# Sixteen modulation tiles per layer change their DMA queue: from SyncE's to ScalarE's, inside the attention of the two mixing layers

## The reference, cut to what matters

```python
c_act = silu(c)
for l in range(2):
    mod = c_act @ w_ada[l] + b_ada[l]                  # (1, 6*1024)
    sh1, sc1, g1, sh2, sc2, g2 = split(mod, 6)
    h = rms_norm(x, norm1_g[l]) * (1 + sc1) + sh1
    q, k, v, iq, ik, iw, z, xbc, dt_raw, ga, gm = split(h @ w_in[l])
    o_attn = dsa_attention(rope(rms(q)), rope(rms(k)), v, iq, ik, iw, 64) @ w_attn_o[l]
    o_ssm = gated_rms(ssd_scan(...)) @ w_ssm_o[l]
    x = x + g1 * ((sigmoid(ga) * o_attn + sigmoid(gm) * o_ssm) @ w_out[l])
    h = rms_norm(x, norm2_g[l]) * (1 + sc2) + sh2
    ...
    x = x + g2 * (ffn(h) @ w_down[l])
```

## Time and profile before

| | |
|---|---|
| three runs | 1649.43, 1653.10, 1655.61 us; median 1653.1 us |
| profiled execution | 1655.45 us, of it span 1653.8 us |
| TensorE / GpSimd / VectorE / ScalarE busy | 96% / 77% / 56% / 52% |
| attention of layer 0, layer 1 (pair 0 to the last transposes) | about 355 to 432 us, 998 to 1070 us from the start |

### The profile page before, as it was taken

The page is one execution under the profiler, slowest core; times in us unless marked ns, Lnnn a source line. Parts: engine busy times, 40 slices in busy tenths (PEclk is TensorE's granted clock), DMA queues, the critical chain, the costliest instruction groups (busy, mean ns, idle before and its releaser), DMA issues.

```text
span 1653.8 us, 33845 instructions
## 1 busy us (share of the span) xinstructions
PE 1593.0 (96%) x13182; PEld 1541.0 (93%) x13182; DVE 925.4 (56%) x1799; ACT 866.3 (52%) x1432; POOL 1271.9 (77%) x948
## 2 busy tenths in 40 slices
PE   7999999999999999999999899999999999999999
PEld 6999988898999999999998899999999998799999
DVE  7767777567646763467677757754442256632200
ACT  3554555554456663465455564545664455655532
POOL 1878967675779999678986767697998786279996
PEclk7999999999999999999999999999999999999999
DMA  8545744446446657455764545654665664146654
GB/s 306 178 146 204 244 165 160 142 166 242 166 141 235 235 200 255 149 156 174 242 207 144 164 155 192 231 178 148 184 190 174 200 202 142 47 152 192 183 188 128
DMA packets 85518, 302.23 MB, mean 183 GB/s; under 512 B 9840, under 2 KB 12528, under 8 KB 85104
## 3 DMA queue, kind: packets, MB, share of 16 engines
q1 hardware_dynamic: 85360, 300.06, 55.3%
HBM read 298.98 MB, written 1.05 MB: 181 GB/s over the span
## 4 chain that ended last, share of the span: by engine, by line
PE 71%; DVE 11%; ACT 5%; DVEq 4%; issue 3%; POOL 2%; DMA 2%; SPq 1%; ACTq 0%; POOLq 0%
PE gemm_bank L1688 63%; ACT w_hi L443 2%; POOL w_lo L425 2%; PE turn_bank L1871 2%; PE turn_bank L1842 2%; DVEq L1337 2%; DVE ada_acc L848 1%; DVE conv L848 1%; DVE h_lo L1383 1%; DVE idx_score L848 1%; DMA ada_first<-in_w_ada 1%; DVE probs L1045 1%; DVEq L1221 1%; PE outp_bank L2078 1%; PE score_bank L1688 1%
## 5 line engine op out<-in xcount | busy, mean ns | idle before, releaser
L425 POOL TENSOR_TENSOR w_lo<-w_raw,w_hi 128x512 fp32r<-128x512 f32 x944 | 1271.7, 1377 | 370.7 <-ACT w_hi L443 357.8
L443 ACT ACTIVATE w_hi<-w_raw 128x1024 fp32r<-128x1024 f32 x472 | 491.7, 1046 | 590.6 <-PE gemm_bank L1688 517.5
L1688 PE MATMUL gemm_bank<-h_hi,w_hi 128*128 128x256 f32 (+1 forms) x2144 | 608.8, 284 | 7.2 <-DVE conv L848 3.7
L1688 PE MATMUL gemm_bank<-h_hi,w_lo 128*128 128x256 f32 (+1 forms) x2144 | 601.2, 280 | 0.0
L1688 PE MATMUL gemm_bank<-h_lo,w_hi 128*128 128x256 f32 (+1 forms) x2144 | 600.8, 280 | 0.0
L1688 PEld LDWEIGHTS gemm_bank<-h_hi,w_hi 128*128 128x128 f32 (+1 forms) x2144 | 403.9, 188 | 16.2 <-issue 7.4
L1688 PEld LDWEIGHTS gemm_bank<-h_lo,w_hi 128*128 128x128 f32 (+1 forms) x2144 | 404.5, 189 | 0.3
L1688 PEld LDWEIGHTS gemm_bank<-h_hi,w_lo 128*128 128x128 f32 (+1 forms) x2144 | 404.0, 188 | 0.2
L848 DVE SCALAR_TENSOR_TENSOR conv<-gemm_bank,params_sb,conv 128x255 f32<-128x255 f32 (+1 forms) x320 | 139.5, 477 | 161.9 <-ACT conv L774 110.7
L1688 PE MATMUL gemm_bank<-w_hi,h_hi 128*128 128x256 f32 (+1 forms) x672 | 193.5, 288 | 2.7 <-DVE h_lo L848 1.5
L1688 PE MATMUL gemm_bank<-w_lo,h_hi 128*128 128x256 f32 (+1 forms) x672 | 188.0, 280 | 0.0
(11 more groups left out here) (310 smaller groups left out, 2165.2 us busy)
## 6 DMA issues: line engine op xcount, KB each, us to landing
w_raw<-in_stream SPq DMA_DIRECT2D x458, 512.0 KB, 3.8
ada_w<-in_w_ada SPq DMA_DIRECT2D x80, 512.0 KB, 4.6
ada_first<-in_w_ada SPq DMA_DIRECT2D x16, 512.0 KB, 12.1
w_raw<-in_stream SPq DMA_DIRECT2D x8, 256.0 KB, 3.1
alibi_sb<-in_alibi SPq DMA_DIRECT2D x1, 1920.0 KB, 7.8
residual<-in_x_t SPq DMA_DIRECT2D x1, 1024.0 KB, 6.7
ada_acc<-in_rows SPq DMA_DIRECT2D x1, 1024.0 KB, 5.1
out_x<-residual SPq DMA_DIRECT2D x4, 256.0 KB, 4.6
```

The costliest lines, as they stand in the source:

```text
L425: ins = nc.gpsimd.tensor_tensor(w_lo[:, s, e], w_raw[:, s, e], w_hi[:, s, e].bitcast(f32), ALU.subtract)
L443: A(w_hi[:, s, 0:n], w_raw[:, s, 0:n], ACT.Copy).then_inc(hi_ready, 1)
L1688: ins = M(o, a, b, start=first and i == 0, stop=last and i == len(passes) - 1, skip_group_check=True)
```

## The change

The sixteen tiles leave SyncE's list and are loaded by ScalarE, two for each pair. The wait that protects the buffer (`ada_used`) goes with each load and now stands in ScalarE's in-order list. Tile 0 is loaded at the head of pair 0, tile 2p+1 at the head of pair p, and tile 2p+2 behind `turn_evac` of pair p (p up to 6). The other tiles of a layer stay on SyncE. Nothing else is changed: same tiles, same buffers, same order of use.

```diff
@@ ada_slots (SyncE's list) @@
             slots = [((U_Z + i, 0), ada_tile(l, "scan", i)) for i in range(8)]
             slots += [(scan_part(h), ada_tile(l, "scan", 8 + h // 4)) for h in range(2, 32, 4)]
-            slots += [(SO_ORDER[min(h, 13)], ada_tile(l, "attention", h)) for h in range(16)]
@@ ScalarE @@
+            def load_attention_tile(l, h):
+                i = ada_tile(l, "attention", h)
+                act.wait_ge(ada_used, i - 1)
+                nc.scalar.dma_start(ada_w[:, i % 2, :], w_ada[i]).then_inc(ada_full[i % 2], 16)
+
             def attention(l):
                 t0 = T_AT if l < DEPTH else T2_AT
                 for p in range(HEADS // 2):
+                    if l < DEPTH:
+                        if p == 0:
+                            load_attention_tile(l, 0)
+                        load_attention_tile(l, 2 * p + 1)
                     head_exp(l, 2 * p)
                     head_exp(l, 2 * p + 1)
...
                     turn_evac(l, 2 * p, t0)
+                    if l < DEPTH and p < 7:
+                        load_attention_tile(l, 2 * p + 2)
```

## The result

The change makes the kernel slower: 1670.03 us (median of four runs, 1668.93 to 1673.64) against 1651.26 us (median of four, 1648.99 to 1655.61), a ratio of 1.0098, 95% interval 1.0064 to 1.0132. The forecast was 1658.0 in a range of 1646 to 1665, made from the first three runs of before (median 1653.1); the time lies beyond it. Of the cases written down, "Clearly slower" (1665) is the nearest.

What follows compares the result with a forecast made beforehand. The prediction took TensorE, busy for 96% of the span, to bound the kernel. Delays of +2.8 us in layer 0 and +2.1 in layer 1 made +4.9, moving the median from 1653.1 to 1658.0 us, range 1646 to 1665.

Steps and rivals of the forecast that it cites:

- Clearly slower: Rival: ScalarE's tiles share DMA engines with freed chunks and take 5 us or more; +12 us, 1665; chance 0.13.
- D: The start of a pair's head maxima on VectorE; the next pair's scores were taken to follow 1.93 us later.
- SyncE's waits go, and give nothing: Both layers: freed chunks win at most TensorE's 0.64 and 1.66 us, swallowed by its wait for the maxima.
- Pair 0 costs nothing: Pair 0: tile 0 lands at about 355.7, wanted from 357.37; cost zero, with 1.7 us to spare.
- The load leaves at D + 0.4: Later pairs: the even tile's load is issued behind the 0.49 us copy `turn_evac`, at about D + 0.4.
- The tile is there 3.8 us after its issue, and only the even tile of a pair counts: Later pairs: tile there at D + 4.2, wanted at D + 2.57; a 1.6 us stall where VectorE starts in time.
- DMA queues: Rule that a second issuing engine saves only issue time: sum 0; kept as a rival, 1653 us, chance 0.12.
- Pair 3 to D of pair 4: No idle time follows pair 3, so D of pair 4 moves +1.1 us in layer 0, +1.6 in layer 1.
- Pairs 1 and 2 take the stall up: VectorE's idle time before D of pair 3, 2.53 and 1.68 us, absorbs the stall; cost 0.
- Pairs 4 to 6: Pair 4: 0; pair 5: 0 in layer 0, +0.4 in layer 1; pair 6 in layer 0: stall 1.6, accumulations +1.0.
- ScalarE's issues: Two issues ahead of a pair's exponentials, 0.8 to 1.7 us, cost 0; as a rival +10 us, 1663, chance 0.05.
- Clock: Within the 0.13 rival: a longer wait lets TensorE's clock fall for a chunk, 2.7 us.

Runs made afterwards that it cites:

- four_act: The change with four tile buffers instead of two, ScalarE asking for tiles a pair ahead; ratio 0.9965 to the kernel before.
- four_sp: The kernel before, tiles still in SyncE's list, with the same four tile buffers in the attention; ratio 0.9968 to the kernel before.
- held_chunks: The change, with SyncE loading six chunks of each attention only once a pair of tiles has landed; ratio 1.0054 to the kernel before.

## Why the prediction was wrong, step by step

Where the two attentions grew, as a change of the time from one D to the next (from the first D to tile 14 in all; one profiled execution each):

| us | pair 0 | pairs 1, 2 | pair 3 | pairs 4 to 6 | behind D of pair 7 | sum |
|---|---|---|---|---|---|---|
| layer 0, forecast | 0 | 0 | +1.1 | +2.6 | -0.9 | +2.8 |
| layer 0, measured | -2.65 | +1.23 | +4.35 | +4.10 | -0.91 | +6.12 |
| layer 1, forecast | 0 | 0 | +1.6 | +0.5 | 0 | +2.1 |
| layer 1, measured | +2.75 | +0.90 | +2.11 | +5.24 | +2.90 | +13.90 |

- **SyncE's waits go, and give nothing.** Right. The 8.40 and 2.04 us of ScalarE went. TensorE's waits for `probsT` of 0.64 and 1.66 us in pair 3 went too, and nothing came of it, since it then waits for the maxima.
- **Pair 0 costs nothing.** Right: tiles 0 and 1 landed in 3.2 and 4.7 us, no wait but for `y_low`, as before.
- **The load leaves at D + 0.4.** Half a microsecond too late: it left at 389.11, with D at 389.21. The issue went out with the start of the copy ahead of it (389.10), not its end. By itself this made the sum too large.
- **The tile is there 3.8 us after its issue, and only the even tile of a pair counts.** This is the step that failed. The 3.8 came from sixteen loads that SyncE had spaced out. On ScalarE two leave 0.4 us apart, together with the chunks that the list now lets go; tiles 2 to 13 landed in 3.6 us at the median in both layers before, and in 4.7 (layer 0) and 5.0 (layer 1) after, with 9.8 and 7.7 at the worst. With it goes something that I left out: of the two tiles of a pair I worked out only the even one, and put the odd one at nothing without a reason. The odd one lands later still, at 5.3 and 6.1 us at the median, and its waits of 3.55 and 3.10 us (before 399.35, and before tile 13 at 1073.13) are as large as any. Over both attentions VectorE waited 24.0 us for tiles, 16.8 for even and 7.2 for odd ones; in the change's second execution 16.2 and 5.4. The run with half the bytes ties size to cause: with landings near my figure the loss was 6.8 us, not 16 to 19.
- **DMA queues.** The Trainium skill (DMA: Bandwidth & Descriptors, Issuing engines are not separate DMA queues) says that loads issued by different engines interleave on the same sixteen DMA engines. The longer landings agree. The time that it would give, no change, holds for four_act and four_sp, 0.9965 and 0.9968, where the asking is equally early on either queue; where the move also changes when a tile is asked for, it doesn't.
- **Pair 3 to D of pair 4.** The right place, +1.1 and +1.6 us forecast; +4.35 in layer 0 (13.2 against 8.9) and +2.1 in layer 1 (10.5 against 8.4). The even tile did what the sum says: there at D + 4.4 and D + 4.0 (forecast D + 4.2), it cost 2.05 and 1.65 us (forecast 1.6), though only because the earlier issue made up for the longer landing. The gap in layer 0 is the odd tile, 3.55 us, and belongs to this execution: in the change's second one tile 7 landed in 5.6 us, cost 0.48, and the next D came 9.5 us after, not 13.2. The accumulations took 3.4 us there, 1.15 less than before where I took 0.5; in layer 1 4.6, 0.6 more. VectorE's timeline of layer 1, tiles 6 and 7, then 13:

```profile
1043.27 4.62 DVE L858 SCALAR_TENSOR_TENSOR ada_acc<-ada_w,c_act,ada_acc 128x1024 f32<-128x1024 f32 x2 [1.65 <-DMA ada_w<-in_w_ada]
...
1073.13 1.28 DVE L858 SCALAR_TENSOR_TENSOR ada_acc<-ada_w,c_act,ada_acc 128x1024 f32<-128x1024 f32 x1 [3.10 <-DMA ada_w<-in_w_ada]
```

- **Pairs 1 and 2 take the stall up.** Right for pair 2: it grew by 0.1 us in either layer, and 3.33 us of VectorE's idle time were left before D of pair 3 in layer 0. Wrong for pair 1, which let 1.1 and 0.8 us through: its tiles landed in 5.9 and 7.0 us in layer 0 and in 4.8 and 6.0 in layer 1.
- **Pairs 4 to 6**: D of pair 4 to D of pair 7 was forecast to grow by 2.6 us in layer 0, all in pair 6, and 0.5 in layer 1, mostly in pair 5. It grew from 19.7 to 23.8 (+4.1) and from 20.0 to 25.3 (+5.2), in all three pairs, by 1.0 to 2.0 us each (pair 5 +1.7 and +2.0, where I had put 0 and 0.4).
- **Pair 0 in the table** is not the change's: the low clock that follows the wait for `y_low` came in layer 0 before and in layer 1 after. The two cancel in the sum of 20.0.
- **Behind D of pair 7** layer 0 came out as forecast. In layer 1 TensorE waited 2.84 us for `probsT`, whose copy stood behind tile 13 and its 3.10 us, and ran at the lower clock from 1078.63 on.
- **ScalarE's issues.** Right: 0.33 us each at the median. The exponentials started 0.85 us after D in pair 3, no later than their maxima allowed.
- **Clock.** I had it as a rival, with 0.13. In the two profiled executions of before and after 9.2 us of the 20.0 are longer busy time of TensorE. It is a step that my sum set to nothing for the likeliest case, though each wait that it predicted to grow (to 2 to 3 us) was of the kind behind which the earlier trace rows show a chunk of 5.49 us. That each such fall comes from a longer wait is argued from times; no run separates the two.
- **Confirmed beside it**: the wait at the scores of pair 5 grew, and no other engine's list took TensorE's time. The mechanism (tiles asked for too late) was right and shown by the move of one load; its size was off by three to four times. The forecast of VectorE's wait for tiles, 1 to 2 us in most pairs, was too low: of pairs 1 to 6 in both layers nine waited, 0.3 to 5.6 us each, and two of them 1 to 2.1 us.

What stays open is the split of the loss, in us of the median, between the partner tile, the freed chunks and the clock: halving bytes acts on all three, holding chunks back gave an unclear trace, and filler matmuls none that can be told. For the landing alone held_chunks gives it: about 1 us of the odd tile's comes with its partner, the rest with chunks.

## What to carry to other kernels

A prefetch that moves to a compute engine's in-order list is issued when that engine gets there, which is a dependence that it did not have: write down for each load when it is asked for and when it is wanted, for every load of a burst and not only the first, and take the landing from loads that share the DMA engines in the way they will. If a list blocks on a full buffer, first ask for more buffers, not another queue: two more tiles gave 0.3% on either queue, where the new queue alone lost 1%. And if a load must stand in such a list, put it ahead of the instruction that waits, not behind.

## What the runs showed of the hardware that I had not expected

- A load of 512 KB, alone 3.2 us, took up to 9.8 us with other tiles and chunks beside it, at a DMA share of 0.57 over the attention. Full DMA engines are not all of it: in one microsecond of that load the share was 0.27, though it and a chunk issued at 391.25 were both still under way (they landed at 399.26 and 399.45). No run says what held them.

```profile
396.00:397.00 1.00, 1.00 (x11) 1.00 (x10) 0.00 (x0) 0.00 (x0) 0.96 (x1) 1.00 0.27 70
```

- ScalarE's DMA issue runs ahead of its compute: with even tiles on ScalarE the load was issued at 384.17, the start of the high half at 384.16, while the copy written between the two started at 385.12. In these rows what held an issue was a wait on a semaphore ahead of it, not work in progress.
- Two executions of one program differ more in such a stretch than its median suggests: the change's attentions took 173.1 and 163.9 us (low clock 30.6 and 17.1 us), those of the early load 152.7 and 157.9.
